# Reordering the RWKV scan step: part of the right-hand side and the next level's first products ahead of a score bank, sample steps at other levels

## What is computed

```
def step(S, inp):                       # per head, N = 64, H = 16 heads
    r_t, w_t, k_t, v_t, kk_t, a_t = inp
    sa = einsum('bhvk,bhk->bhv', S, -kk_t)
    S = (S * w_t[:, :, None, :] + sa[..., None] * (kk_t * a_t)[:, :, None, :]
         + v_t[..., None] * k_t[:, :, None, :])
    return S, einsum('bhvk,bhk->bhv', S, r_t)
S, y = lax.scan(step, S0, (r, decay, k, v, kk, a))
```

## Time and profile before

| what | value |
|---|---|
| median of 3 runs | 3019.54 us |
| the 3 runs | 3018.93, 3019.54, 3026.66 us |
| the profiled execution | 3016.34 us |
| its span, first to last instruction | 3014.3 us, so 2.04 us lie around it |
| mean granted TensorE clock | 0.979 |
| the scan (16 steps) | about 914 to 1121 us of the span |
| one step, mean over w = 1 to 14 | 12.58 us |

### The profile page before, as it was taken

The page is one execution under the profiler, slowest core; times in us unless marked ns, Lnnn a source line. Parts: engine busy times, 40 slices in busy tenths (PEclk is TensorE's granted clock), DMA queues, the critical chain, the costliest instruction groups (busy, mean ns, idle before and its releaser), DMA issues.

```text
span 3014.3 us, 72962 instructions
## 1 busy us (share of the span) xinstructions
PE 2876.1 (95%) x29617; PEld 2733.3 (91%) x29617; DVE 1528.4 (51%) x2080; ACT 1085.0 (36%) x2139; POOL 1321.5 (44%) x959
## 2 busy tenths in 40 slices
PE   6999999998989999999998999999999999899998
PEld 5998999997978877899997899889999899799998
DVE  3435666118357874666603242476650444566612
ACT  4224333225455652433323444343332422433322
POOL 3443444442435554344443273434444344344443
PEclk9999999999999999999999999999999999899999
DMA  7544333544411013333354323533334543133332
GB/s 269 164 151 159 95 92 88 158 128 136 119 44 32 4 37 124 120 89 92 99 159 152 99 64 112 169 123 89 92 116 146 173 120 91 57 92 92 91 91 85
DMA packets 465618, 332.56 MB, mean 110 GB/s; under 512 B 19914, under 2 KB 435608, under 8 KB 465122
## 3 DMA queue, kind: packets, MB, share of 16 engines
q1 hardware_dynamic: 461400, 325.24, 35.1%
q10 hardware_dynamic: 4010, 4.22, 0.6%
HBM read 319.62 MB, written 10.20 MB: 109 GB/s over the span
## 4 chain that ended last, share of the span: by engine, by line
PE 62%; DVE 4%; ACT 2%; issue 1%; DMA 1%; SPq 0%; POOL 0%; ACTq 0%; DVEq 0%
PE banks L1667 33%; PE banks L1675 16%; PE banks L2126 5%; PE banks L2133 1%; PE banks L1628 1%; PE banks L1973 1%; DVE h L2662 1%; PE banks L1690 1%; DVE proj L2606 1%; PE banks L1761 0%; DMA s_state<-in_state_wkv_b_dram 0%; ACT conv L1080 0%; PE banks L2135 0%; ACT uv L1433 0%; DVE proj_b L2606 0%
## 5 line engine op out<-in xcount | busy, mean ns | idle before, releaser
L765 POOL TENSOR_TENSOR w_lo<-w_raw,w_hi 128x1024 fp32r<-128x1024 f32 x395 | 1007.5, 2551 | 1108.1 <-ACT w_hi L981 1088.0
L1667 PE MATMUL banks<-u_hi,w_hi 128*128 128x260 f32 x4064 | 834.5, 287 | 14.2 <-ACT w_hi L981 9.4
L1667 PE MATMUL banks<-u_lo,w_hi 128*128 128x260 f32 x4064 | 825.1, 284 | 0.0
L1667 PEld LDWEIGHTS banks<-u_hi,w_hi 128*128 128x128 f32 x4064 | 627.4, 189 | 27.1 <-issue 15.2
L1667 PEld LDWEIGHTS banks<-u_lo,w_hi 128*128 128x128 f32 x4064 | 629.9, 189 | 1.6
L981 ACT ACTIVATE w_hi<-w_raw 128x1024 fp32r<-128x1024 f32 x402 | 424.5, 1056 | 454.2 <-PE banks L1675 284.4
L1675 PE MATMUL banks<-u_hi,w_lo 128*128 128x260 f32 x4064 | 527.5, 282 | 0.0
L1675 PEld LDWEIGHTS banks<-u_hi,w_lo 128*128 128x128 f32 x4064 | 502.1, 187 | 1.3
L1667 PE MATMUL banks<-hid_hi,w_hi 128*128 128x260 f32 x1664 | 336.3, 283 | 0.0
L1667 PE MATMUL banks<-hid_lo,w_hi 128*128 128x260 f32 x1664 | 335.2, 283 | 0.0
L3113 DVE TENSOR_TENSOR csb<-proj 128x520 f32 (+1 forms) x42 | 30.3, 722 | 470.8 <-ACT proj L1048 470.8
(11 more groups left out here) (463 smaller groups left out, 3898.8 us busy)
## 6 DMA issues: line engine op xcount, KB each, us to landing
w_raw<-in_ffn_w_up_dram SPq DMA_DIRECT2D x176, 512.0 KB, 3.7
ada_raw<-in_ada_w_dram SPq DMA_DIRECT2D x96, 512.0 KB, 4.7
w_raw<-in_ffn_w_down_dram SPq DMA_DIRECT2D x64, 448.0 KB, 3.7
w_raw<-in_sconv_w_in_dram SPq DMA_DIRECT2D x48, 512.0 KB, 5.2
ada_ahead<-in_ada_w_dram SPq DMA_DIRECT2D x36, 512.0 KB, 7.7
ada_ahead_down<-in_ada_w_dram SPq DMA_DIRECT2D x36, 512.0 KB, 6.2
w_raw<-in_ffn_w_down_dram SPq DMA_DIRECT2D x32, 512.0 KB, 4.0
ada_pro<-in_ada_w_dram SPq DMA_DIRECT2D x6, 2048.0 KB, 21.2
```

The lines of the kernel that those rows point to most:

```text
L765: pool.tensor_tensor(w_lo[:, s, :, :], w_raw[:, s, :, :], w_hi[:, s, :, :].bitcast(F32), ALU.subtract).then_inc(lo_done, 1)
L1667: pe.matmul(tile_ps[slot][half][0:width, 0:HALF], w_hi[:, s, k, 0:width], x[:, k0 + k, half * HALF:(half + 1) * HALF], start=start and k = ...
```

## The change

It has four parts, all in the scan step.

1. PE: `right_side(q, (0, 1))`, with its wait for `st_updated`, moves from behind the first products of level 1 to right behind the updates of level 0, ahead of `outputs_of_solution` and `state_products`.
2. PE: `first_products` of level 1 moves ahead of the first score bank (n = 0) of the next step.
3. DVE: the sample operations move. Step q = 0 has j = 0, 1 after level 0, j = 2 after level 1 and j = 3 at the end; step q = 1 has 4, 5 then 6 then 7, 8. Before, it was 0 after level 1 and 1, 2, 3 at the end; 4 after level 1 and 5 to 8 at the end.
4. DVE: the last mask moves ahead of `receptances`.

No instruction is added or removed.

```diff
@@ PE, scan_step
                         update_products(w, q, 0)
+                        pe.wait_ge(st_updated, w + 1)
+                        right_side(q, (0, 1))
                         if w:
                             outputs_of_solution(w - 1, qn)
                             state_products(qn)
+                        first_products(w, q, 1)
                         if one_more:
                             scores_among(w + 1, qn, 0)
                             scores_of_keys(w + 1, qn, 0)
                         for lvl in range(1, NLV):
-                            first_products(w, q, lvl)
-                            if lvl == 1:
-                                pe.wait_ge(st_updated, w + 1)
-                                right_side(q, (0, 1))
+                            if lvl > 1:
+                                first_products(w, q, lvl)
@@ DVE, scan_step
-                        samples = (((0,), (1,), (2, 3)), ((4,), (5, 6), (7, 8)))[q]
+                        samples = (((0, 1), (2,), (3,)), ((4, 5), (6,), (7, 8)))[q]
...
-                            if lvl == 1:
-                                for j in samples[0]:
+                            if lvl < 2:
+                                for j in samples[lvl]:
                                     sample_state(c, j)
...
+                        if one_more:
+                            mask_scores(w + 1, 1 - q, 3)
                         if two_more:
                             dve.wait_ge(y_mm, 2 * w + 1)
                             receptances(c + 1, q)
-                        if one_more:
-                            mask_scores(w + 1, 1 - q, 3)
...
-                        for j in samples[1]:
-                            sample_state(c, j)
                         for j in samples[2]:
                             sample_state(c, j)
```

## The result

| | before | after |
|---|---|---|
| median of 14 runs each | 3019.51 us | 3030.25 us |
| their range | 3017.09 to 3026.66 | 3023.31 to 3035.47 |
| profiled execution (span) | 3016.34 (3014.3) | 3029.57 (3027.5) |
| mean granted TensorE clock | 0.979 | 0.979 |

The changed kernel is slower: ratio 1.0035, 95% interval 1.0028 to 1.0042, 10.7 us. The forecast was 3022.3 us with a range of 3013 to 3029, so it was wrong.

A forecast was written before the change was run, and what follows sets the result against it. PE was busy 95% of the span, but DVE's list ahead of level 1 would be late. +5.2 - 2.8 + 0.9 - 0.5 = +2.8 us on 3016.34 gave 3019.1; 3.2 more for the median: 3022.3 us, range 3013 to 3029.

The forecast's parts named there:

- Part 1, the slot: PE ahead of the outputs: the right-hand side fills 0.37 us of idle time per step, at most 5.5 us in all.
- Part 2, first products 0.82 us earlier: PE and POOL ahead of level 1: first products and POOL's `ct` come 0.82 us earlier, level 1's updates up to 0.37.
- Part 3: DVE ahead of level 1: two sample operations and meetings with POOL make it 0.45 us late; +5.2 us in fourteen steps.
- PE's order gives back 0.06 to 0.1 us: PE at level 2's first products: its order recovers 0.06 to 0.1 us of DVE's delay; 0.08 taken, leaving 0.37 a step.
- Part 4, the mask: Ahead of `turn_inverse`: the earlier mask lets PE start it 0.2 us sooner in each of 14 steps, -2.8 us.
- Step 0 and the end: Step 0: score bank now behind PE's wait, +0.9 us (0 to +1.5); behind step 15: -0.5 us (-1.5 to +0.5).
- The slower rival: DVE between state's update and level 2: all three meetings with POOL, mask's gain lost; +0.7 a step, 3030.3 us; chance 0.11.
- hardly meet: Rival: POOL's `ct` fall between DVE's operations, level 1's 0.10 delay is hidden, only the mask counts; 3016.6 us; chance 0.26.
- the +0.4: Term in the rival sum 0 - 2.8 + 0.4 - 0.5 = -2.9 us, written beside the end's -0.5.

The follow-up runs named there:

- part 3 alone: The kernel before with only the sample operations on DVE moved as in the change: 3026.63 us, ratio 1.0024.
- part 4 alone: The kernel before with only the last mask moved ahead of `receptances`: 3019.56 us, ratio 0.9997.
- the kernel before with short `ct`: The kernel before, with POOL writing only 4 of 64 columns of the masked blocks `ct` of levels 1 and up: 3019.26 us, ratio 0.9996.
- all but part 3: The changed kernel with the sample operations back where they stood before: 3018.92 us, ratio 0.9992.
- part 2 undone: The changed kernel with one sample operation ahead of the state's update, and first products of level 1 behind the score bank again: 3018.15 us, ratio 0.9995.
- one ahead: The changed kernel with one sample operation ahead of the state's update, one behind level 1, the others at the step's end: 3013.70 us, ratio 0.9983.

## Why the prediction was wrong, point by point

- **Part 1, the slot.** Right: the idle time ahead of `sc,uv` is gone in all 15 steps and PE waits for DVE's `mmt` in its place.
- **Part 2, first products 0.82 us earlier.** Right: 1.08 instead of 1.90 us behind the outputs. That POOL's `ct` come earlier too was right (1.62 instead of 2.50); what they hit then was not. I wrote that they meet the copy and the first sample operation and that `L2936` (now L2937) isn't held, since it starts 0.03 us ahead. It starts 0.03 us behind and is held by 0.28 us, while the sample operation behind the copy isn't.
- **Part 3: this is the step that failed.** The part that was mis-sized is DVE's list, and the part left out is the meeting with `build` (next point). The list from the update to level 1 was put at 2.46 us with nothing in the way and 2.81 with POOL. It took 3.19. Of the 0.73 us over 2.46, the meetings are 0.42 (0.28 and 0.14), where I had charged 0.35; the rest, 0.32, is that the two waits, put at "some 0.04 us" each, are 0.24 and 0.16. Most of that rest is not the price of a wait as such. DVE's steps 1 to 12 are in a hardware loop, steps 0 and 13 to 15 are written out, and there the same waits are 0.10 and 0.03 us. In step 13 of the changed kernel:

```profile
1091.29 0.31 DVE L2922 COPY end_decay<-bd_Ep 128x4 f32<-128x4 f32 x1
1091.71 0.69 DVE L2885 TENSOR_TENSOR s_state<-s_state,s_tmp 128x512 f32<-128x512 f32 x1
1092.43 0.69 DVE L2887 TENSOR_TENSOR s_tmp<-s_vec 128x512 f32<-128x512 f32 x1
```

  Level 1 starts 4.14 us behind the outputs there, against 4.39 in step 7. The looped steps' surplus, 0.13 and 0.13 us in 12 steps, is by estimate 3.1 us of the loss. Why the loop adds it was not tested. The trace of before has both kinds of wait in its loop: 0.04 and 0.03 us ahead of two of the sample operations at the end of step 7, which bear the forecast's figure out, and 0.15 ahead of the last, a row that I did not read:

```profile
1017.05 0.69 DVE L2890 TENSOR_REDUCE s_vec<-s_tmp 128x512 f32 x1 [0.15 <-DVE s_tmp L2888]
```

- **"PE's order gives back 0.06 to 0.1 us."** Nothing was given back behind level 1. I also had DVE's stretch from level 2 to level 3 unchanged; the later level moves `build` onto POOL's inverse, +0.16 us a step. The path up to level 3 grew by 0.87 us a step (12.2 us in 14), where I had 0.37 (5.2 us) and a bound of 10.2.
- **Part 4, the mask.** The 0.2 us came (0.19 a step, from level 3 to the next outputs, 2.7 us), but not from the mask: with part 3 alone, which has the mask in its old place, the same stretch is already down to 4.61 us, against 4.56 in most steps of the changed kernel and 4.78 in most of the kernel before. With level 3 that late, the mask is hardly waited for. The term had the right size and for the most part the wrong cause, which is luck; the run of part 4 alone shows it in clean steps only.
- **Step 0 and the end.** +1.32 for +0.9 and -0.44 for -0.5, both within their bounds.
- **The rivals.** The slower rival had the place right, and its +0.7 us a step was measured as 0.68. Its prices were others: two meetings and not three, waits on DVE that it did not have, and `build` held instead of the operation behind level 1, behind which 0.37 us of idle time are left. I gave it 0.11 because it wanted all meetings at once. The program repeats every step, so meetings that the order brings about fall alike in every step: it was one event and not several. In "hardly meet" the -0.5 of the end is taken twice (it is in the +0.4 already): -2.4 and 3017.1 us are meant, which changes nothing in the forecast.

The Trainium skill ("SBUF — State Buffer", section "SBUF: two separate sides") calls the shared pair of ports an exclusive lock for the whole instruction, held by whoever starts first. The runs agree in part. A DVE operation that starts 0.03 us behind a `ct` is held, one that starts 0.05 us ahead of it isn't; but one that starts 0.01 us ahead of the inverse is held too (`L2906`), and one that starts 0.29 us behind a `ct`, which is 0.45 us long, takes 0.71 us, hardly more than alone (step 8 of the changed kernel, 1025.35). No operation was held for a whole `ct`: 0.28 and 0.31 us are the most in the stretches shown.

## What to carry to other kernels

Before an operation is moved into idle time of its engine, ask whether that idle time lies ahead of or behind the operation that the other engines wait for: the same 0.7 us cost nothing ahead of the state's update and 0.5 us behind it. An engine that is made to start earlier (here POOL's `ct`) can land on another's critical operations; lay its new times over the neighbour's list and charge every overlap in each step, since a loop makes them fall alike. Price a chain of operations that wait for each other on one engine by the distance of their starts in the trace, not by the duration of one, and read it in the same surroundings: the same two waits cost 0.26 us more inside DVE's hardware loop than outside it.

## What the runs showed of the hardware

- **Operations on DVE that wait for the one before.** Two independent operations of 0.41 us start 0.33 us apart (1018.54 and 1018.87 in step 7 of the changed kernel); two of 0.42 us of which the second waits start 0.45 us apart (1010.63 and 1011.08). For operations of 0.69 us in the written-out steps it is 0.72 us with a wait (1091.71, 1092.43) and 0.61 without (1092.43, 1093.04). So a wait costs 0.11 to 0.12 us of distance. In the looped steps 0.85 us lie between the same two (1012.37, 1013.22), 0.13 more. The Trainium skill ("Perfetto Trace Analysis", section "DVE / Act Engine Instruction (TENSOR_ADD, Activation, etc)") lets the next instruction begin to fetch when the first has finished in the engine, while its semaphore goes out only once the write is acknowledged; the trace agrees in kind, with the 0.11 to 0.12 us between the two. It doesn't say why the loop adds 0.13.
- **A meeting slows both.** The two `ct` took 1.05 us in the changed kernel, where they met the update and the copy, and 0.88 in the kernel before. With 4 of the 64 columns, POOL still took 0.54 us for two beside the update, and 0.43 where they met nothing (at 1008.83 in the kernel before with short `ct`), so about half of the 0.88 us doesn't shrink with the columns. Yet they held DVE by 0.03 us instead of 0.28.
- **Waits of PE on "issue"** of 0.2 to 0.8 us (time in which PE waited for nothing that the profile shows) come at up to seven places of a traced scan: 7 in all but part 3 and in part 2 undone, 2 in the changed kernel, 3 in one ahead, none in part 3 alone. Their cause stays open; no run was made on it.
